# Paged decode attention inside a decoder layer: keys turned by VectorE in 32x32 blocks and scored by 32x32 TensorE tiles, in rounds of eight pages, all keys ahead of all values

## The reference, cut to what matters

```python
def diff_attend(q, k, v, q_pos, k_pos, lam):
    s = jnp.einsum('bqhmd,bkhmd->bhmqk', q, k) * (DK_A ** -0.5)       # 4 heads, m = 2 halves of 64
    mask = k_pos[None, :] <= q_pos[:, None]
    p = jax.nn.softmax(jnp.where(mask, s, -jnp.inf), axis=-1)
    w = p[:, :, 0] - lam * p[:, :, 1]
    return jnp.einsum('bhqk,bkhd->bqhd', w, v)

def attend_paged(q, k, v, lam, cache_k, cache_v, page_table):
    pk = cache_k[page_table].reshape(DB, P, H_A, 2, DK_A)            # 8 x 2048 x 4 x 128
    pv = cache_v[page_table].reshape(DB, P, H_A, DV_A)
    k_all = jnp.concatenate([pk, k], axis=1)
    v_all = jnp.concatenate([pv, v], axis=1)
    return diff_attend(q, k_all, v_all, P + jnp.arange(T), jnp.arange(P + T), lam)
```

## Time and profile before

| | |
|---|---|
| median of 3 runs | 981.8 us (981.21 to 983.45) |
| profiled execution, span | 982.1 us |
| PE busy in the span | 921.5 us (94%), 6995 products and transposes |
| DVE busy | 489.7 us (50%) |
| ACT busy | 391.1 us (40%) |
| DMA moved | 142.36 MB |
| attention stage | 457 to 731 us |

### The profile page before, as it was taken

How to read it: one execution, slowest core, us unless ns; L and a number is a source line. 1 busy time by engine, 2 the same in 40 slices (tenths; PEclk the granted TensorE clock), 3 DMA queues, 4 the chain that set the end, 5 groups by cost and what they waited for, 6 DMA issues and landing times.

```text
span 982.1 us, 18543 instructions
## 1 busy us (share of the span) xinstructions
PE 921.5 (94%) x6995; PEld 736.8 (75%) x6995; DVE 489.7 (50%) x1081; ACT 391.1 (40%) x840; POOL 108.5 (11%) x233
## 2 busy tenths in 40 slices
PE   4989989999999999998899999999779999999996
PEld 3989979999888888887566667766557886677774
DVE  4634745555574355454476655556474443533213
ACT  5533353433334643434544544455462222421211
POOL 1300000000000000003000023332020000000000
PEclk9999999999999999999999999999899999999998
DMA  7362215222332222223967679968885422213221
GB/s 220 105 175 65 65 45 150 66 65 66 102 102 72 86 65 66 86 65 93 394 221 236 230 253 342 346 229 284 289 281 194 161 86 70 65 32 118 75 91 43
DMA packets 115266, 142.36 MB, mean 145 GB/s; under 512 B 9623, under 2 KB 75799, under 8 KB 115178
## 3 DMA queue, kind: packets, MB, share of 16 engines
q1 hardware_dynamic: 109418, 122.31, 38.8%
q0 software_dynamic: 5760, 18.88, 5.5%
HBM read 125.34 MB, written 15.41 MB: 143 GB/s over the span
## 4 chain that ended last, share of the span: by engine, by line
PE 82%; DMA 5%; DVE 4%; ACT 3%; SPq 3%; issue 2%; POOL 0%; POOLq 0%; ACTq 0%; DVEq 0%
PE ps L1962 71%; PE ps L1965 10%; DMA Vr<-in_cache_v 3%; DMA Kr<-in_cache_k 2%; DMA xrow<-in_x_prompt 1%; SPq L589 1%; PE ps L1957 1%; SPq L564 1%; DVE pp L1776 0%; ACT wh L952 0%; ACT junk L1231 0%; ACT whi L911 0%; DVE kTs L1741 0%; SPq L480 0%; DMA g<-in_state_m 0%
## 5 line engine op out<-in xcount | busy, mean ns | idle before, releaser
L1962 PE MATMUL ps<-hhi,whi 128*128 128x272 f32 (+1 forms) x672 | 228.3, 340 | 1.2 <-DVE hlo L1296 1.2
L1962 PE MATMUL ps<-hhi,wlo 128*128 128x272 f32 (+1 forms) x672 | 218.8, 326 | 0.0
L1962 PE MATMUL ps<-hlo,whi 128*128 128x272 f32 (+1 forms) x672 | 218.5, 325 | 0.0
L1962 PE MATMUL ps<-wh,r 128*128 128x512 f32 (+1 forms) x544 | 155.4, 402 | 0.7 <-DVE wout_lo L1842 0.6
L1962 PEld LDWEIGHTS ps<-hhi,whi 128*128 128x128 f32 x672 | 128.6, 191 | 13.9 <-issue 3.7
L1962 PEld LDWEIGHTS ps<-hlo,whi 128*128 128x128 f32 x672 | 128.8, 192 | 9.9 <-issue 1.9
L1962 PEld LDWEIGHTS ps<-hhi,wlo 128*128 128x128 f32 x672 | 128.5, 191 | 9.2
L1962 PEld LDWEIGHTS ps<-wh,r 128*128 128x128 f32 (+1 forms) x544 | 99.4, 185 | 27.1 <-issue 1.9
L1312 DVE TENSOR_TENSOR wlo<-wst,whi 128x1024 fp32r<-128x1024 f32 x56 | 68.8, 1229 | 81.7 <-ACT whi L911 81.7
L1741 DVE COPY kTs<-ps 128x512 f32<-128x512 f32 x64 | 44.1, 690 | 66.2 <-PE ps L1965 66.1
L1965 PEld LDWEIGHTS ps<-ident,Kr 128*128 128x128 f32 x512 | 56.1, 141 | 25.3 <-issue 22.5
(11 more groups left out here) (355 smaller groups left out, 1331.9 us busy)
## 6 DMA issues: line engine op xcount, KB each, us to landing
Kr<-in_cache_k SPq DMA_DIRECT2D x128, 256.0 KB, 4.2
wst<-in_w_in SPq DMA_DIRECT2D x56, 512.0 KB, 3.8
Vr<-in_cache_v POOLq DMA_DIRECT2D x72, 256.0 KB, 4.7
Vr<-in_cache_v SPq DMA_DIRECT2D x56, 256.0 KB, 4.2
out_y_prompt<-rows SPq DMA_DIRECT2D x16, 512.0 KB, 2.9
xrow<-in_x_prompt SPq DMA_DIRECT2D x8, 512.0 KB, 4.9
wout<-in_w_out SPq DMA_DIRECT2D x8, 512.0 KB, 5.7
rows<-in_x_prompt SPq DMA_DIRECT2D x8, 512.0 KB, 4.3
```

What stands on the lines that cost most here:

```text
L1962: return nc.tensor.matmul(out, lhsT, rhs, start=start, stop=stop, **more)
```

## The change

Keys are no longer turned by PE. DVE turns each key step's two pages in place, by one transpose of 128x1024 that turns each 32x32 block by itself (`keys_turned`). A block then has 32 dims on partitions and 32 tokens in columns. PE scores four key steps at once (a round, `scores(g)`): 64 products of a 32x32 weight with 256 columns, on 16 tiles of the array (4 groups of 32 rows by 4 of 32 columns), into banks 0 to 3, summed over rounds. The queries are spread to all four row groups by 16 small products (`q_spread`), an ACT copy (`q_rep`) and 8 POOL copies for each batch (`own_queries`). DVE stores a whole batch at its end, 4 times 512 columns (`scores_out`). The new tokens' scores come first, from `q_new`.

`Kr` has room for 8 steps, `Vr` with half of `Kr` for 8 value steps. Even steps are issued by SP, odd ones by POOL. All 64 key steps come before all 64 value steps; steps follow the estimated PE cost of the positions, the first 45% of it for the keys. `WOUT_AT` puts all parts of the weight behind unit 15. ACT has no key copies left. Cut to its core, in the order SP, POOL, DVE, ACT, PE behind the tables:

```diff
+ROUND = GROUPS // 2
+ROUNDS = KEY_STEPS // ROUND
+IN_ROUNDS = ROUNDS // BATCHES
+RING = 2 * ROUND
+STORE_STEP = tuple(round_step(IN_ROUNDS * (b + 1) - 1) + 1 for b in range(BATCHES))
+EXP_STEP = tuple(n + 1 for n in STORE_STEP)
+VALUE_STEP = [(KEY_STEPS + 4, KEY_STEPS + 6)[m // IN_BATCH] + m for m in range(KEY_STEPS)]
-LATE = [cost + 0.3 for cost in ATTEND]
+PACE = [cost + 0.3 for cost in ATTEND]
+KEY_SHARE = 0.45
 for pos in range(POSITIONS):
...
+    if n < AO_STEP[1]:
+        share = sum(PACE[2:pos + 1]) / sum(PACE[2:VALUES_END + 1])
+        if share < KEY_SHARE:
+            n = int(VALUE_STEP[0] * share / KEY_SHARE + 0.001)
+        else:
+            n = VALUE_STEP[0] + int((AO_STEP[1] - VALUE_STEP[0]) * (share - KEY_SHARE) / (1 - KEY_SHARE) + 0.001)
-WOUT_AT = [1, 3, 5, 7, 17, 20, 23, 26]
+WOUT_AT = {15: 2, 17: 3, 19: 4, 21: 5, 23: 6, 25: 7, 27: 0, 28: 1}
...
+        def value_slot(q, k):
+            return Vr[:, GP * (q % ROUND) + k, :] if q % RING < ROUND else Kr[:, GP * (q % ROUND) + k, :]
...
             def key_pages(n):
-                if n >= 4:
-                    sp.wait_ge(s["k_used"], n - 3)
+                if n >= RING:
+                    sp.wait_ge(s["scores_ready"], n // ROUND - 1)
...
+            for n in range(1, RING, 2):
+                key_pages(n)
+            nc.gpsimd.memset(qk[0][:], 0.0).then_inc(s["zero_ready"], 1)
+            def own_queries(b):
+                for m in range(2):
+                    for j in range(PACK):
+                        nc.gpsimd.tensor_copy(own, spread_q[:, 2 * m:2 * m + 2, :, PACK * b + j, :]
+                                              ).then_inc(s["q8_ready"], 1)
...
+            def keys_turned(n):
+                dve.wait_ge(k_in[n % RING], 16 * GP * (n // RING + 1))
+                pair = Kr[:, GP * (n % RING):GP * (n % RING) + GP, :].rearrange("p k d -> p (k d)")
+                nc.vector.transpose(pair, pair).then_inc(s["k_turned"], 1)
+            def scores_out(b):
+                dve.wait_ge(s["scores_ready"], IN_ROUNDS * (b + 1))
+                for a in range(4):
+                    out = S[b][:, 0:PAST].rearrange("p (g t) -> p g t", t=PAGE)[:, :, 32 * a:32 * a + 32]
+                    nc.vector.tensor_scalar(out, ps[:, a, :].rearrange("p (g t) -> p g t", t=32), 1.0, LOWEST,
+                                            ALU.mult, ALU.max, accum_out=gmax[:, a:a + 1]).then_inc(s["s_stored"], 1)
...
             def decode(n):
-                    nc.vector.tensor_copy(kTs[:, n % 2, 2:4, :], ps[:, 1, :].rearrange("p (h k) -> p h k", h=2)
-                                          ).then_inc(s["kT_dve"], 1)
+                    keys_turned(n)
...
             def decode(n):
-                if n < KEY_STEPS:
-                    copy(kTs[:, n % 2, 0:2, :], ps[:, 0, :].rearrange("p (h k) -> p h k", h=2), "kT_act")
...
-            def keys(n):
-                        for k in range(GP):
-                            last = turn(ps[:, half, (h * GP + k) * P:(h * GP + k + 1) * P],
-                                        Kr[:, GP * (n % 4) + k, (2 * half + h) * P:(2 * half + h + 1) * P])
+            def scores(g):
+                b, r = divmod(g, IN_ROUNDS)
+                j, half = divmod(r, 2)
+                pe.wait_ge(s["k_turned"], ROUND * (g + 1))
+                if r == 0:
+                    pe.wait_ge(s["q8_ready"], NSEQ + 2 * PACK * (1, 3)[b])
+                    if b:
+                        pe.wait_ge(s["s_stored"], 4 * b)
+                pages = slice(GROUPS * half, GROUPS * half + GROUPS)
+                for c in range(H):
+                    for h in range(H):
+                        for a in range(4):
+                            rows = slice(32 * a, 32 * a + 32)
+                            first = h * DH + 32 * c
+                            last = mm(ps[32 * h:32 * h + 32, a, 256 * half:256 * half + 256].rearrange("p (g t) -> p g t", t=32),
+                                      qk[b][rows, j, h, c, :], Kr[rows, pages, first:first + 32],
+                                      r == 0 and c == 0, r == IN_ROUNDS - 1 and c == H - 1, skip_group_check=True)
+                last.then_inc(s["scores_ready"], 1)
+            def turn_weights(b, t):
+                pe.wait_ge(s["s_stored"], 4 * BATCHES)
...
             def decode(n):
-                if n < KEY_STEPS:
-                    keys(n)
-                if 1 <= n <= KEY_STEPS:
-                    scores(n - 1)
+                if n == 1:
+                    new_scores()
+                if n % ROUND == 0 and ROUND <= n <= KEY_STEPS:
+                    scores(n // ROUND - 1)
```

More of the change, by code:

```diff
@@ L105 @@
 TURNS_AT = {n: [bt for bt in TURNS if TURN_STEP[bt] == n] for n in range(STEPS_OF_DECODE)}
-FIRST_VALUES = [20 + 3 * q for q in range(4)]
-VALUES_BY_SP = 36
-AHEAD = 4
+VALUE_ISSUE = [KEY_STEPS - 2 * ROUND + 1 + q if q < RING // 2 else round_step(ROUNDS - 2) + 1 + q - RING // 2 if q < RING
+               else VALUE_STEP[q - RING] + 1 for q in range(KEY_STEPS)]
+VALUES_ISSUED_AT = {n: [q for q in range(KEY_STEPS) if VALUE_ISSUE[q] == n] for n in range(STEPS_OF_DECODE)}
 PHASES = 4
@@ L573, in _ @@
[L573 to L587 removed]
+                if n % RING == 0:
+                    own_pages(n)
@@ L593, in _ @@
             sp.wait_ge(s["piece_done"], EVENTS)
-            for n in range(4):
+            for n in range(0, RING, 2):
                 key_pages(n)
@@ L626, in _ @@
                         allow_slow_non_contiguous=True)
-                if pos == at(15, 0):
-                    page[:] = [None] * GROUPS
-                    for four in range(VALUES_BY_SP // 4, VALUES_BY_SP // 4 + AHEAD):
-                        load_value_pages(four)
                 if turn_at == 14:
@@ L823, in _, with own_pages @@
             pool.wait_ge(s["masks_ready"], 8)
-            nc.gpsimd.memset(q8[:], 0.0).then_inc(s["zero_ready"], 1)
-            pool.wait_ge(s["zero_ready"], 16 + 4)
+            pool.wait_ge(s["ptab_in"], PTAB_IN)
+            ck = io["cache_k"][0].rearrange("n p h d -> n p (h d)")
+            cv = io["cache_v"][0].rearrange("n p h d -> n p (h d)")
+            page = [None] * RING
+            def own_pages(first):
+                page[:] = nc.values_load_multi_w_load_instructions(
+                    ptab[0:1, first:first + RING], engines=[mybir.EngineType.Pool], min_val=0, max_val=POOL - 1)[1]
@@ new lines, in key_pages @@
+            def key_pages(n):
+                if n % RING == 1:
+                    own_pages(KEY_STEPS + n - 1)
+                if n >= RING:
+                    pool.wait_ge(s["scores_ready"], n // ROUND - 1)
+                for k in range(GP):
+                    nc.gpsimd.dma_start(Kr[:, GP * (n % RING) + k, :],
+                                        ck[bass.ds(page[n % RING // 2 * GP + k], 1), :, :].rearrange("o p d -> (o p) d")
+                                        ).then_inc(k_in[n % RING], 16)
@@ new lines, in value_pages @@
+            def value_pages(q):
+                if q % RING == 1:
+                    own_pages(3 * KEY_STEPS + q - 1)
+                if q < RING:
+                    pool.wait_ge(s["scores_ready"], IN_ROUNDS if q < ROUND else ROUNDS - 1)
+                else:
+                    pool.wait_ge(s["v_used"], q - RING + 1)
+                for k in range(GP):
+                    nc.gpsimd.dma_start(value_slot(q, k),
+                                        cv[bass.ds(page[q % RING // 2 * GP + k], 1), :, :].rearrange("o p d -> (o p) d")
+                                        ).then_inc(v_in[q % RING], 16)
@@ L1088, in _ @@
             evict(EVENTS - 1)
+            act.wait_ge(*done["q_spread"])
+            copy(q_rep[:, :, :, :], ps[:, 0, :].rearrange("p (c h t) -> p c h t", c=H, h=H), "q_rep_stored", scale=QSCALE)
             act.wait_ge(s["bo_done"], CH)
@@ L2362, in head_values @@
                     pe.wait_ge(s["on_ready"], users[-1] + 1)
+                if bank == 0 and h == 0:
+                    pe.wait_ge(s["s_stored"], 4 * BATCHES)
                 tile = tile_of(u)
```

284 lines of the change are left out of this document (127 added, 157 removed).

## The result

The changed kernel took 991.5 us in the median of 4 runs (990.42 to 998.0), the kernel before 982.6 beside it (981.21 to 986.83, 4 runs). The ratio is 1.0079, with an interval of 1.0048 to 1.0111: slower by 0.8%, 8 to 9 us. The profiled execution spans 988.8 us against 982.1.

What follows compares the result with a forecast made beforehand. PE's list was taken to set the pace up to unit 15, then PE, pages and the chain of short units together. Against the profiled 982.1 us, +13 - 27 + 3 + 5 = -6 gave 976 us; range 953 to 1008.

Steps and rivals of the forecast that it cites:

- A: The forecast itself, summed over the stretches: 976 us, with the middle of each range 966 to 988; chance 0.42.
- Positions 0 to 7: The stretch before unit 0, 24.4 us in the kernel before: a change of 0, between -3 and +5 us.
- The transpose: DVE's 64 transposes of 128x1024: 1.22 us each, 78 us in all; 1.15 as lower end, 2.3 at half rate.
- Rival D: DVE's block transpose goes at half rate, 2.3 us each: 68 us more, 1040 us; chance 0.08.
- The round: PE's 16 rounds of 64 products: 2.1 us each, 34 us in all, relieving PE of 68 us.
- E: PE's row groups don't run together: 7.2 us a round, 1003 us; chance 0.05.
- The pages' loop: Half rings load only behind their round: issue and landing 0.3 + 4.2 us; missed pages cost 10 us over 14 rounds.
- Units 0 to 9: DVE becomes the bound: 112 us of work plus 12 idle, 124 us for 111.1: +13, range +3 to +30.
- Units 10 to 15: Keys leave this stretch, 41 us for 68.4: -27; an open softmax in front adds +3 (1 to 6).
- Units 16 to the end: 40 value steps instead of 34, and their pages crowded behind the keys: 75 us for 70.1, +5 (-5 to +14).
- C: DVE waits for pages in every round, 34 us idle instead of 12: 998 us; chance 0.20.
- B: DVE hardly ever idle, no open softmax, deeper ring takes the waits: -30 at most, some 958 us; chance 0.22.

Runs made afterwards that it cites:

- the run with one block: The changed kernel with rounds multiplying only the first of four blocks of dims, 16 products a round instead of 64: 970.9 us, ratio 0.9868.

## Why the prediction was wrong

Forecast were 976 us and faster; it was 991.5 and slower, within the range of 953 to 1008 and outside A's own of 966 to 988. By its own steps:

**Positions 0 to 7** (0): right within the scatter, unit 0 at 481.3 for 481.4.

**The transpose** (1.22 us): right, 1.225. My estimate of 1.24 from the figure in the Trainium skill (VectorE: DVE Perf Modes, The three transpose paths) agrees as well. Rival D is out.

**The round** (2.1 us): this term was mis-sized. The row groups do run together, so E is out, but a round takes longer. A round at the lower and one at the upper level of the clock (1.2 and 2.4 GHz; the granted clock of the two is 0.50 and 1.00), from PE's timeline:

```profile
498.25 4.53 PE L2012 MATMUL ps<-Kr,qk 32*32 32x256 f32 x128 [1.84 <-DVE Kr L1740]
...
516.20 2.76 PE L2012 MATMUL ps<-Kr,qk 32*32 32x256 f32 x128 [0.83 <-DVE Kr L1740]
```

The 14 rounds in units 0 to 9 are between these, 48.0 us in all, 3.4 each instead of 2.1, 18.6 us more. Seven of the 14 are 2.76; that is 0.66 above the forecast in each, 9.2 us in 14. Its rows start over 2.4 us (516.2 to 518.6), where I had four blocks of 0.43 each, 1.7: that price was too low, also with 16 tiles side by side. Of the other 9.4 us, 8.7 are in six rounds that lie wholly or partly at the lower level, 0.6 in one of 3.37 us at a granted clock of 1.00, whose cause I did not find. Four of the five longest, 4.06 to 4.53, come behind 1.8 to 4.9 us in which PE stood idle. An estimate by the factor of 10.6 for 16 tiles in the Trainium skill (TensorE: Matmul & The Clock Gate, Part 3: Packing small matmuls) gave 3.0 us; the round at the upper level is 2.76, a little under it and nearer to it than to my 2.1. By the run with one block, whose rounds are 0.73 to 1.17 us (some 0.9, so 35 us of rounds less), at least half of a change of the rounds reaches the time. Half of 18.6 is 9 us, an estimate, and most of the 11 by which this stretch was missed.

**The pages' loop** (0.3 + 4.2 us): mis-sized too. Landing took 5.4 and 6.0 us in the median, not the 4.2 of the earlier trace rows; eight DMAs go out together now. In the run with half of the keys' pages the medians were 2.8 and 4.1. Page waits were 16.3 us for my 10, and taking them away gave 8.

**Units 0 to 9** (+13, measured +24.2): this is the step that failed. DVE's work was forecast at 112 us and was 105.2: 55 keys lie in the stretch, not 56 to 58, and one store instead of two. Its idle time was forecast at 12 us and was 30.1. I had counted idle time as misses of one engine, with a place each. The waits show a loop of all: pages wait for the round, the turn for the page, the round for the turn, the next minima for the scores behind the round. With nearly no turning it needs 121 us, with a short round 117, with half the pages 127, and with all three parts in place 135. No part is the bound alone, and each gives back only a part of what is taken from it: 14 of 54 us, 18 of 35, 8 of 12. That these parts carry time is shown by the runs; how much of the 18 us of idle time above the forecast is longer rounds, how much late pages and how much the order of the lists is not.

**Units 10 to 15** (-27 + 3 = -24, measured -16.6): too large by 7 us. PE has 42.1 us of work there, where I had 36 and a round (the 36 take the keys from the stretch's 68.4 us; from PE's busy 66.4 they leave 34); the chain of 41 us for the six units was an estimate from no row. Units 11 to 15 took 37.8 us (7.6 each), unit 10, with the last round and the open softmax, 14.0. The open softmax shows as one wait of ACT for DVE's maxima, in the waits of 616.6 to 630.6 us:

```profile
ACT S L1166 <- DVE small L1764: 8.1, 1, 8.1
```

How much of unit 10 it costs was not tried.

**Units 16 to the end** (+5, measured -0.8): the pages bind as forecast (share 0.93; 24.2 MB are 70.5 us at 344 GB/s), only the amount was put too high: I had 25 MB and no lead of the ring.

**The sum.** 11.2 us too little in units 0 to 9, 7.4 too much gain behind, 5.8 too much loss in the last stretch: 12.8 us, the way from -6 to +6.7. Nearest of the rivals in mechanism is C, which had 34 us of idle time in place of 12 and 998 us. Its point of decision, 18 us of idle time, was right and was passed. Its mechanism was half of it: DVE waited for pages at 7 turns, not in every round, and most of the other 13.8 us for PE. What spoke for a larger sum was in my own working: three hand-overs between lists in each of 14 rounds, and 12 us for all of them, 0.3 us each. B needed a DVE that is hardly ever idle, and is 33 us off. E's time of 1003 us is near too, but its rounds of 7.2 us are not there.

Left open: what the clock's lower level costs by itself. No run kept PE busy in its waits. The forecast had 10 us for it in the range. In the rounds of units 0 to 9 it is about 9 us, and the units' own products there took 4.9 us longer than before (scores 23.7 for 21.6, weights times values 16.9 for 15.4, turns of the weights 11.5 for 10.2), at a granted clock of 0.86 for 1.00. That is 14 us of PE's time, of which an unknown part shows: a rival for some of the 11 us that no run tested.

## What to carry to other kernels

When a change moves work from the engine that binds to one that has just enough room, don't just add up the new engine's work and a few misses. Draw the loop that the change closes (load, turn, multiply, free the buffer, load) and count each hand-over between lists in fixed order, for there each engine's other work gets into the loop; a stretch with two engines at 72 and 78% and a DMA at 68% took 24 us longer here than the one before with an engine at 96%. Then spread that loop over the stretches that have slack: moving 7 of 55 keys back gave 7 us, more than any of the repairs tried in the loop itself, and six keys more lost it again behind, at a DMA share of 0.97.

## What the runs showed of the hardware

64 products of 32x32 tiles with 256 columns of 32-bit values, 16 tiles side by side, took 2.76 us at the upper level of the clock and 4.53 at the lower, a factor of 1.64 and not 2.

An in-place 32x32 block transpose of 128x1024 32-bit values took 1225 ns on DVE, as long as a two-input operation of that size (1229 ns), so a 4-byte type does not halve its rate.

Pages landed late behind a small DMA. The DMA of `out_n_prompt`, 4-byte elements, was issued at 532.0 us; POOL's page of 532.3 landed 12.3 us later, the longest of all, and while it was under way the DMA moved 49 GB/s at a share of 0.43:

```profile
538.00:544.50 6.50, 2.96 (x22) 1.97 (x20) 2.83 (x6) 2.64 (x5) 2.15 (x4) 1.00 0.43 49
```

With all three outputs of the state (this one, m, and C of 256 KB) behind the decode no landing of a page in that place took over 7.0 us, and of the page waits of 3.8 and 4.4 us one of 1.1 was left.
